# TensorE waits for its own last tile three times per feed-forward, and the 272-column rows start at other addresses

## The reference, cut to what matters

```python
for l in range(DEPTH):                     # first block, 272 rows
    h = h + 0.5 * swiglu(rms_norm(h, ffn1_norm[l]), ffn1_w_gu[l], ffn1_w_down[l])
    u = rms_norm(h, mix_norm[l])
    ... = split_cols(u @ w_in[l], IN_SPLITS)      # attention and recurrent inputs, gates
    merged = jax.nn.sigmoid(ga) * y_a + jax.nn.sigmoid(gb) * y_b
    h = h + merged @ w_out[l]
    h = h + 0.5 * swiglu(rms_norm(h, ffn2_norm[l]), ffn2_w_gu[l], ffn2_w_down[l])
return rms_norm(h, final_norm)[:, N_META:]
...
for l in range(DEPTH):                     # second block, 256 rows
    x = macaron_ffn(x, ...)                # rms_norm, swiglu, rms_norm of the result
    m = recurrent_block(...) if l == 0 else moba_attention(...) @ attn_w_o
    x = x + rms_norm_2(m, mix_post_g[l])
    x = macaron_ffn(x, ...)                # after layer 0 also keys and values
```

## Time and profile before

| | us |
|---|---|
| median of 3 runs | 2376.81 |
| lowest, highest | 2365.05, 2380.16 |
| the profiled execution | 2368.04 |
| its span | 2366.3 |
| mean granted TensorE clock in it | 0.976 |

### The profile page before, as it was taken

One profiled execution on the slowest core, in us unless ns is written; L12 is line 12 of the kernel. 1 busy time (PEld: TensorE's weight loads), 2 busy tenths in 40 slices (PEclk: granted clock), 3 DMA queues, 4 the chain that ended last, 5 costly groups with the idle time before them and its releaser, 6 DMA issues.

```text
span 2366.3 us, 49110 instructions
## 1 busy us (share of the span) xinstructions
PE 2246.4 (95%) x18270; PEld 2206.1 (93%) x18270; DVE 1398.5 (59%) x1966; ACT 1161.2 (49%) x1752; POOL 555.6 (23%) x589
## 2 busy tenths in 40 slices
PE   7999999999999999999999999985999999978998
PEld 7999988999999999888999899985999999978998
DVE  6555866655555557756565555476664655465553
ACT  5444544454345436444454455466554545455553
POOL 4322000232213220001332242024431132111420
PEclk9999999999999999999999999997999999998999
DMA  6554423455546545233565466442565556532663
GB/s 210 186 188 154 149 90 117 141 170 171 184 142 195 187 157 166 87 98 117 161 199 192 141 197 200 156 161 89 179 211 169 195 179 199 176 114 87 200 203 116
DMA packets 99258, 380.47 MB, mean 161 GB/s; under 512 B 10911, under 2 KB 13087, under 8 KB 99016
## 3 DMA queue, kind: packets, MB, share of 16 engines
q1 hardware_dynamic: 99144, 378.91, 49.5%
HBM read 377.80 MB, written 3.16 MB: 161 GB/s over the span
## 4 chain that ended last, share of the span: by engine, by line
PE 86%; DVE 6%; ACT 3%; issue 2%; DVEq 1%; POOL 1%; DMA 0%; ACTq 0%; SPq 0%
PE bank L607 26%; PE bank L608 25%; PE bank L609 25%; ACT whi L1000 2%; PE bank L667 2%; DVE wlo L1399 2%; PE bank L668 2%; PE bank L669 2%; PE bank L884 1%; PE bank L625 1%; PE bank L794 1%; PE bank L873 0%; DVE cv L1735 0%; PE bank L863 0%; POOL outlo L2042 0%
## 5 line engine op out<-in xcount | busy, mean ns | idle before, releaser
L1399 DVE TENSOR_TENSOR wlo<-raw,whi 128x1024 fp32r<-128x1024 f32 (+1 forms) x660 | 869.6, 1329 | 528.2 <-ACT whi L1000 525.8
L1000 ACT ACTIVATE whi<-raw 128x1024 fp32r<-128x1024 f32 (+1 forms) x660 | 729.2, 1117 | 439.9 <-PE bank L609 401.9
L607 PE MATMUL bank<-x_tokens_hi,wlo 128*128 128x256 f32 x1784 | 498.7, 280 | 4.3 <-DVE z L1751 3.6
L608 PE MATMUL bank<-x_tokens_lo,whi 128*128 128x256 f32 x1784 | 497.1, 279 | 0.0
L609 PE MATMUL bank<-x_tokens_hi,whi 128*128 128x256 f32 x1784 | 497.1, 279 | 0.0
L607 PEld LDWEIGHTS bank<-x_tokens_hi,wlo 128*128 128x128 f32 x1784 | 338.9, 190 | 5.9 <-issue 3.8
L608 PEld LDWEIGHTS bank<-x_tokens_lo,whi 128*128 128x128 f32 x1784 | 336.3, 189 | 0.0
L609 PEld LDWEIGHTS bank<-x_tokens_hi,whi 128*128 128x128 f32 x1784 | 336.0, 188 | 0.0
L1980 POOL TENSOR_TENSOR z<-sil,z 128x256 f32<-128x256 f32 (+1 forms) x176 | 176.4, 1002 | 567.7 <-DVE z L1443 416.3
L609 PE MATMUL bank<-hid_tokens_hi,whi 128*128 128x256 f32 x880 | 244.7, 278 | 0.0
L607 PE MATMUL bank<-hid_tokens_hi,wlo 128*128 128x256 f32 x880 | 244.6, 278 | 0.0
(11 more groups left out here) (378 smaller groups left out, 4958.7 us busy)
## 6 DMA issues: line engine op xcount, KB each, us to landing
raw<-ffn_gu SPq DMA_DIRECT2D x352, 512.0 KB, 3.7
raw<-ffn_down SPq DMA_DIRECT2D x128, 704.0 KB, 4.1
raw<-mix SPq DMA_DIRECT2D x120, 512.0 KB, 3.5
raw<-rec SPq DMA_DIRECT2D x28, 512.0 KB, 3.9
raw<-kv SPq DMA_DIRECT2D x16, 512.0 KB, 4.4
raw<-att SPq DMA_DIRECT2D x16, 512.0 KB, 3.9
bias_rows<-rows SPq DMA_DIRECT2D x8, 256.0 KB, 4.3
bias<-bias_rows SPq DMA_DIRECT2D x1, 1536.0 KB, 9.0
```

The source lines that it names most:

```text
L607: pe.matmul(out, wlo[:, slot, w], xh(i), start=(i == 0), stop=False)
L608: pe.matmul(out, whi[:, slot, w], xl(i), start=False, stop=False)
L1000: act.activation(whi[:, k, 0:cols], raw[:, k, 0:cols], ACT.Copy).then_inc(hi_made, 1)
L1399: dve.tensor_tensor(wlo[:, k, 0:cols], raw[:, k, 0:cols], whi[:, k, 0:cols].bitcast(F32), ALU.subtract).then_inc(lo_made, 1)
```

## The change

Before the loop of gate and up tiles TensorE waits until its own eighth tile is done; the loop is cut into turns 2 and 3 and turns 4 to 10, with a wait for tile 16 between them; a third wait, for tile 44, stands before the down products. This holds in all eight feed-forwards. The rows of 272 columns get other places: modulo 256, inputs of layer 0 at 160, 32 (mixer) and 128, of layer 1 at 96 and 0 (mixer); hidden rows at 224 and 96 in layer 0, 32 in layer 1. The 256-column arrays stay at 64. The space held for the arrays grows by 64 bytes each, and what lies behind them moves by as much.

```diff
-        LINE, SHIFT, BACK_SHIFT, ROW = 256, 64, 192, T + 48
+        LINE, SHIFT, ROW = 256, 64, T + 48
...
-        X = {0: pair_at("x_first", KD, xbase + SHIFT, ROW), 1: pair_at("x_mixer", KD, xbase + SHIFT, ROW),
-             2: pair_at("x_second", KD, xbase + BACK_SHIFT, ROW), "last": x_tokens, "F4": x_tokens, "REC": x_tokens,
-             "F5": x_tokens, "F6": x_tokens, "ATT": x_tokens, "F7": x_tokens}
-        top[0] = xbase + BACK_SHIFT + 2 * KD * ROW * 4
+        X = dict.fromkeys(("last", "F4", "REC", "F5", "F6", "ATT", "F7"), x_tokens)
+        X.update({0: pair_at("x_first", KD, xbase + 160, ROW), 1: pair_at("x_mixer", KD, xbase + 32, ROW),
+                  2: pair_at("x_second", KD, xbase + 128, ROW), "late": pair_at("x_late", KD, xbase + 96, ROW),
+                  "late_mixer": pair_at("x_late_mixer", KD, xbase, ROW)})
+        top[0] = xbase + LINE + 2 * KD * ROW * 4
...
-        HID = {0: pair_at("hid_first", KF, hbase + SHIFT, ROW), 2: pair_at("hid_second", KF, hbase + BACK_SHIFT, ROW),
-               "last": hid_tokens, "F4": hid_tokens, "F5": hid_tokens,
-               "F6": hid_tokens, "F7": hid_tokens}
-        hid_end, ebase = hbase + BACK_SHIFT + 2 * KF * ROW * 4, hbase + BACK_SHIFT + 2 * KF * SEQ * 4
+        HID = dict.fromkeys(("last", "F4", "F5", "F6", "F7"), hid_tokens)
+        HID.update({0: pair_at("hid_first", KF, hbase + 224, ROW), 2: pair_at("hid_second", KF, hbase + 96, ROW),
+                    "late": pair_at("hid_late", KF, hbase + 32, ROW)})
+        hid_end, ebase = hbase + LINE + 2 * KF * ROW * 4, hbase + LINE + 2 * KF * SEQ * 4
...
-                        f=l * 2 + which // 2, c=N_META if (l, which) == (DEPTH - 1, 2) else 0, layer=True, s="last" if (l, which) == (DEPTH - 1, 2) else which)
+                        f=l * 2 + which // 2, c=N_META if (l, which) == (DEPTH - 1, 2) else 0, layer=True,
+                        s=which if l < DEPTH - 1 else ("late", "late_mixer", "last")[which])
...
-        AFTER = {0: 1, 2: 0, "last": "F4"}
+        AFTER = {0: 1, 2: "late", "late": "late_mixer", "last": "F4"}
...
-                with pe.Fori(2, FFN_GU_QUADS) as b:
-                    for k in range(RING):
-                        k8_tile(b + q, k, b * RING + j + k - 3, k, X[s], c)
+                for first, end in ((2, 4), (4, FFN_GU_QUADS)):
+                    pe.wait_ge(tile_done, first * RING + j)
+                    with pe.Fori(first, end) as b:
+                        for k in range(RING):
+                            k8_tile(b + q, k, b * RING + j + k - 3, k, X[s], c)
...
+                pe.wait_ge(tile_done, j + 2 * KF)
                 with pe.Fori(0, FFN_DOWN_QUADS if layer else FFN_DOWN_QUADS - 1) as b:
                     down(b)
...
-                        first_tiles(q, 2, X[1], 0, inputs_ready(x), input_norm(x, n, 0))
+                        first_tiles(q, 2, X[st["s"]], 0, inputs_ready(x), input_norm(x, n, 0))
...
-                        hi, lo, at_k = sources.get(TILE[t][0], (*X[1], 0))
+                        hi, lo, at_k = sources.get(TILE[t][0], (*X[st["s"]], 0))
```

## The result

| | before | after |
|---|---|---|
| median of 8 runs each, us | 2374.56 | 2396.44 |
| lowest, highest | 2365.05, 2386.32 | 2390.66, 2403.20 |
| the profiled execution | 2368.04 | 2403.04 |
| its span; mean granted clock | 2366.3; 0.976 | 2401.2; 0.978 |

The ratio is 1.0098, 95% interval 1.0072 to 1.0123. The prediction was 2363 us, range 2338 to 2388, with 0.08 on slower by over 1% and 0.58 on within 1%: the median lies 8 us above the range, and the ratio at the upper edge of that last class. The two profiled executions are 35.0 us apart, the medians 21.9. That these two differ so much is itself part of the finding.

The account below looks back on a forecast made before the run. TensorE, busy 95% of the span, was taken as the bound: matmul count times pace, plus gaps. From 2368.0 us, -12.5 (repair), +16.0 (waits), -5.4 (second feed-forward) and -2.9 (late mixer) gave 2363 us, range 2338 to 2388.

Parts of the forecast that it names:

- What a wait costs: Eight feed-forwards: TensorE waits cost 0.60 us ahead of L711 (16 times), 0.80 us ahead of L729 (8 times), +16.0 us.
- The rival of the cheap wait: Added waits cost as little as the stop at L625, giving 2355 us; chance 0.10.
- What the waits repair: 256-column feed-forwards `last` and F6: matmuls behind the first wait return from 117.8 to 113.3 ns, -12.5 us together.
- the stop doesn't bring the quick pace: Rival: stops fail to restore 113.3 ns, or a near miss takes it away again; 2376 us, chance 0.09.
- The second feed-forward leaves 192: Layer 0's second feed-forward, 1584 matmuls: starts 128 and 96 instead of 192 bring 123.3 ns, -5.4 us; ends -10.6 and 0.
- the middle: Pace assumed for 272-column matmuls at new row starts: 123.3 ns, between 120.0 and 126.6.
- The other rows: Both layers' first feed-forwards and the mixers, 272 columns, leave start 64: sum 0, ends -15.2 and +15.1 us.
- the two rivals on the starts: New 272-column starts better than the middle, 2343 us, chance 0.28; or worse, slower than before, 2384 us, chance 0.15.
- the worse one: Rival: any 272-column start but 64 has 13.3 ns on top, 2384 us; decides from 125.5 ns average; chance 0.15.
- The start doesn't matter: Rival: row starts have no effect, stages differ by how they were entered; 2371 us, chance 0.05.
- The late mixer's 256-column tiles: Second layer's mixer, 480 matmuls on tokens alone: start moves from 128 to 64, 119.4 to 113.3 ns, -2.9 us.
- The base: The sum started from the one profiled execution of the kernel before, 2368.0 us, 8.8 below the median of 2376.8.

## Why the prediction was wrong, step by step

**What a wait costs: right.** 0.60 and 0.80 us were predicted from MOVE, the sequencer's instructions and the late second matmul; 0.61 and 0.79 stand in the trace, +16.1 against +16.0. The cover named, a sequencer ahead of the array, was gone as said. The rival of the cheap wait is out.

**What the waits repair: the step that failed.** It said that "a full stop brings the quick pace back", worth -12.5 us. Behind the 70 stops at loops in the 256-column stages of seven traces (15 each in the changed kernel's two and with the waits alone, 5 each in the two with the first wait and the one with the third, 10 with two waits) 31 parts are quick and 39 slow: 4, 6 and 10 of 15, 1, 0 and 0 of 5, 10 of 10. Quick ones fall slow at a stop with the third wait alone in five cases of five. So a stop settles the pace anew, and not always to the quick one.

These are not 70 separate draws. With the waits alone and with two waits, all five stages of a trace came out alike at each stop. And the gap goes with the outcome to the nanosecond: sorted by stop and by the pace ahead of it, no length stands on both sides.

| stop, pace ahead | gap where slow behind, ns (cases) | gap where quick behind, ns (cases) |
|---|---|---|
| first, quick | 620, 621 (15) | 622, 651 (9) |
| first, slow | none | 624, 625, 627, 654 (6) |
| second, quick | 616 (4) | 617 (10) |
| second, slow | 619 (5) | 649 (1) |
| third, quick | 822, 823, 852, 853 (10) | 821 (1) |
| third, slow | 825 (5) | 826, 827 (4) |

No run sets the gap on purpose, so this is no cause shown: gap and pace may both follow from something that the traces don't name.

In the profiled pair the step is +11.4 in place of -12.5, 23.9 of the 40 us between forecast and trace. The evidence was one stop in the recurrent stage, one draw that came out quick; and the earlier trace rows, stages that were slow in this execution, were taken for a property of the program to be repaired. The same trace held a case against it. F6 itself begins behind a stop, of 0.57 us from the last matmul ahead of it:

```profile
1890.66 0.38 PE L928 MATMUL bank<-consts,z 128*128 128x128 f32 x2
1891.34 0.44 PE L928 MATMUL bank<-consts,z 128*128 128x128 f32 x2 [0.30 <-DVE z L1791]
```

Behind it come the slow tiles of the earlier trace rows. That TensorE never stands in F6 is right, but the stop just ahead of it was left out of account. The prediction's rival "the stop doesn't bring the quick pace", 2376, at 0.09, named the mechanism but priced it as no change, not as a draw that can also lose.

By the medians it is milder. 21.9 us, interval 17 to 29, less 16.1 for stops and 3.7 for the rows leave -3 to +9: what the draws cost the average run of the changed kernel is not resolved. It is resolved for the first wait alone (7 to 22 us above its price), for the third (2 to 17) and for two waits with the rows at 64 (13 to 29 us measured, 9.8 - 5.3 = 4.5 priced). In the average run of those three, stops made the quick pace rarer; why stays open.

**The second feed-forward leaves 192: half right.** -2.2 instead of -5.4: 125.3 ns at 128 and 96, not the 123.3 taken as the middle.

**The other rows: mis-sized.** 0 was taken, +6.4 measured in the feed-forwards (125.7 at 160, 126.7 at 224, 125.3 at 96, 123.3 at 32), and +1.4 in the late mixer's 272-column tiles. "Middle" was made to be the best pace known, so it had room only above. Of the two rivals on the starts, the worse one was nearer: it was to decide from an average of 125.5 ns, and the feed-forward rows average (2 x 125.7 + 126.7 + 3 x 125.3 + 2 x 125.3 + 123.3) / 9 = 125.3, by thirds of 528; with the mixers' 936 matmuls at 123.3 and 456 at 126.7 it is 125.1. "The start doesn't matter" is out.

**The late mixer's 256-column tiles: right in size.** 73 in 8 us against 69, though the slow pace comes there too; -1.9 measured, -2.9 said.

**The base.** The sum stood on one trace at 2368.04 whose five stages had drawn some two fifths slow. The range took in errors of terms, not that before and after are each a draw of up to 36 us. As a ratio, the fixed terms alone, 16.1 + 3.7 on 2374.6, are 1.0083: inside the measured interval.

## What to carry to other kernels

If a stretch has two paces, take a second trace of the unchanged kernel before explaining which stage has which: a mend that is read from one execution may mend nothing. Before a rule is taken from one stop, look at every other stop of the same trace. Stopping a queue that runs ahead costs the sequencer's whole way to the next load, 0.6 to 0.8 us here, and is only worth that where the state behind it is known. Where weights and moving rows are read together, try their distance modulo 256 bytes first; 272 columns had 3.4 ns between best and worst, and one array can be moved in place of many.

## What the runs showed that was not expected

- The pace of back-to-back matmuls depends on where rows and weights lie to each other, not on the rows' own address alone: 651 or 634 in 80 us for rows that did not move.
- At distances 64 and 192, 256 columns have 113.3 or 117.8 ns, at 160 116.7 or 117.8, at 32 117.3 or 118.7. At 64 two traces each of three kernels show that the execution draws which; without a stop it is mostly held to the end of the down products; 272 columns have one pace at each distance, 224 excepted. The granted clock is 1.00 in all of it.
- The pace can fall without a stop: `last` at 1175.40 in the kernel before, F6 at 1912.59 in its second trace, F7 between 2210 and 2211 with inputs at 192. Each time it is two tiles into the loop of L711, where one interval is 0.15 to 0.17 us. Feed-forwards without added stops that come in quick and stay quick have 0.13 to 0.16 us at the same place, so it is a draw too.
- The pace behind a stop goes with the gap's length to the nanosecond, in all 70 stops. What makes both is open; the releaser doesn't, and at 0.01 us the gaps look the same.
